# Expert tiles of a mixture-of-experts kernel: projections in native fp32 on two halves of the array, without splits

## What is computed

```python
D_MODEL, SEQ, N_EXPERTS, TOP_K_EXPERTS, EXPERT_FF = 1024, 256, 32, 2, 512
for e in range(N_EXPERTS):
    hid = jax.nn.silu(t @ w_gate[e]) * (t @ w_up[e])
    out = out + combine[:, e:e + 1] * (hid @ w_down[e]).astype(F32)
```

## Time and profile before

| | |
|---|---|
| median of three runs (least, most) | 2270.79 us (2269.74, 2271.43) |
| span of the profiled execution; its own time is not given apart | 2268.9 us |
| PE busy | 2194.2 us, 97% |
| DVE busy | 1573.7 us, 69% |
| ACT busy | 1168.7 us, 52% |
| POOL busy | 90.1 us, 4% |
| moved by DMA | 496.88 MB, mean 219 GB/s |

### The profile page before, as it was taken

The page is one execution under the profiler, slowest core; times in us unless marked ns, Lnnn a source line. Parts: engine busy times, 40 slices in busy tenths (PEclk is TensorE's granted clock), DMA queues, the critical chain, the costliest instruction groups (busy, mean ns, idle before and its releaser), DMA issues.

```text
span 2268.9 us, 26611 instructions
## 1 busy us (share of the span) xinstructions
PE 2194.2 (97%) x9804; PEld 1610.6 (71%) x9804; DVE 1573.7 (69%) x1576; ACT 1168.7 (52%) x1185; POOL 90.1 (4%) x79
## 2 busy tenths in 40 slices
PE   7989996999999999999999999999999999999999
PEld 5435765655665665565888887888888888878887
DVE  6989558888888878886555883855465558756554
ACT  4124524676666666665433585553354346665332
POOL 2750000000000000000000000000000000000000
PEclk9989997999999999999999999999999999999999
DMA  6224343999999999995555543555455544435653
GB/s 235 93 75 135 108 178 134 353 371 361 358 364 365 369 361 363 366 367 217 194 195 167 172 159 117 204 186 171 164 192 197 195 159 162 155 130 169 205 183 112
DMA packets 166451, 496.88 MB, mean 219 GB/s; under 512 B 10272, under 2 KB 21792, under 8 KB 136400
## 3 DMA queue, kind: packets, MB, share of 16 engines
q1 hardware_dynamic: 164528, 491.70, 60.8%
q10 hardware_dynamic: 1616, 3.24, 0.4%
q0 software_dynamic: 208, 0.59, 0.1%
HBM read 494.45 MB, written 1.05 MB: 218 GB/s over the span
## 4 chain that ended last, share of the span: by engine, by line
PE 82%; DVE 11%; issue 3%; ACT 3%; POOL 0%; DMA 0%; DVEq 0%; ACTq 0%; POOLq 0%
PE ps L1025 20%; PE ps L1035 15%; PE ps L1034 15%; PE ps L1511 9%; PE ps L1492 5%; PE ps L1496 5%; PE ps L1193 3%; PE ps L1480 2%; PE ps L1549 1%; DVE W_r L2859 1%; DVE xn L2582 1%; PE ps L1161 1%; PE ps L1162 1%; DVE W L2587 1%; ACT w_hi L2051 1%
## 5 line engine op out<-in xcount | busy, mean ns | idle before, releaser
L2398 DVE TENSOR_TENSOR w_lo<-raw,w_hi 128x2048 fp32r<-128x2048 f32 (+2 forms) x153 | 336.1, 2208 | 136.6 <-ACT w_hi L1830 129.4
L1830 ACT ACTIVATE w_hi<-raw 128x2048 fp32r<-128x2048 f32 (+2 forms) x153 | 281.6, 1849 | 227.3 <-PE ps L1025 194.1
L1035 PE MATMUL ps<-w_hi,a_lo 128*128 128x512 f32 (+1 forms) x984 | 371.6, 378 | 0.0
L1025 PE MATMUL ps<-w_hi,a_hi 128*128 128x512 f32 (+1 forms) x936 | 356.9, 381 | 0.2 <-DVEq L2438 0.2
L1034 PE MATMUL ps<-w_lo,a_hi 128*128 128x512 f32 (+1 forms) x928 | 349.5, 377 | 0.0
L1035 PEld LDWEIGHTS ps<-w_hi,a_lo 128*128 128x128 f32 x984 | 185.2, 188 | 34.6
L1025 PEld LDWEIGHTS ps<-w_hi,a_hi 128*128 128x128 f32 x936 | 176.2, 188 | 33.1 <-issue 2.1
L1034 PEld LDWEIGHTS ps<-w_lo,a_hi 128*128 128x128 f32 x928 | 174.8, 188 | 30.8
L1492 PE MATMUL ps<-w_hi,W_r 128*128 128x512 f32 x468 | 189.5, 405 | 4.3 <-DVE raw_r L2859 3.4
L2398 DVE TENSOR_TENSOR y_lo<-raw,y_hi 128x2048 fp32r<-128x2048 f32 x51 | 116.9, 2291 | 51.2 <-ACT y_hi L1830 48.6
L1830 ACT ACTIVATE y_hi<-raw 128x2048 fp32r<-128x2048 f32 x51 | 97.8, 1917 | 72.7 <-PE ps L1025 63.1
(11 more groups left out here) (468 smaller groups left out, 4325.5 us busy)
## 6 DMA issues: line engine op xcount, KB each, us to landing
raw<-in_w_in SPq DMA_DIRECT2D x56, 1024.0 KB, 5.1
raw<-in_ffn_w_gate SPq DMA_DIRECT2D x44, 1024.0 KB, 5.1
raw<-in_ffn_w_up SPq DMA_DIRECT2D x44, 1024.0 KB, 5.1
raw<-in_ffn_w_down SPq DMA_DIRECT2D x40, 1024.0 KB, 6.2
raw<-in_w_up SPq DMA_DIRECT2D x30, 1024.0 KB, 8.2
raw<-in_w_gate SPq DMA_DIRECT2D x30, 1024.0 KB, 7.2
lo_f<-in_w_up SPq DMA_DIRECT2D x30, 1024.0 KB, 8.1
lo_f<-in_w_down SPq DMA_DIRECT2D x29, 1024.0 KB, 7.9
```

Source lines behind the costliest of these rows:

```text
L1025: return released(pe.matmul(dst, a, b, skip_group_check=True, **kw))
L1035: return pe.matmul(dst, a_l, b_h, start=False, stop=final, skip_group_check=True)
L1830: act.activation(E.hi_view(name, ahead), E.raw_view(name, ahead), ACT.Copy).then_inc(hi_split, 1)
L2398: tt(E.lo_view(name, ahead), E.raw_view(name, ahead), E.hi_view(name, ahead).bitcast(F32), ALU.subtract)\
```

## The change

Gate and up are computed as down is: native fp32 products straight from the raw units. The 512 columns of a unit's block are cut in two halves of 256; the first goes to rows 0 to 63 of the bank and the second to rows 64 to 127, with the same 64 stationary columns at array position 0 and 64. Gate and up share one bank (columns 0 to 255 and 256 to 511). Down does the same with its two halves of 512 columns. All splits of expert weights go, and with them `lower_half` and `halves_added`. sil_e and hid_e become 128 rows of 256; two transposes turn them. A period gathers two blocks in one bank with one copy. `spread` and the output parts have two buffers, cleared once by POOL, and a tile is scattered two periods later (PE: `scatter_before`). Loads follow the order gate, up, down of one tile; the count of 8 buffers and of units stays.

```diff
-MOE_RAW, MOE_HI = 8, 4
+MOE_RAW = 8
...
+            def expert_gate_up(k, name, group, q):
+
+                dst = bank(name)
+                for i, kind in enumerate("gu"):
+                    for half in range(2):
+                        w = landed(((kind, k), half))
+                        for j in range(4):
+                            a = packed_rows[group][:, 4 * half + j, q, :]
+                            for side, rows in enumerate((lower_rows, upper_rows)):
+                                at = 512 * j + SEQ * side
+                                m = pe.matmul(dst[rows, SEQ * i:SEQ * i + SEQ], a, w[:, at:at + SEQ],
+                                              start=i == half == j == 0, stop=i == half == 1 and j == 3,
+                                              skip_group_check=True, tile_position=(0, SLOTS * side))
+                        if (kind, half) != ("u", 1):
+                            m.then_inc(expert_used, 1)
+                fill(m, name)
...
+                    w = landed((("d", k), half))
+                    for r in range(2):
+                        for c, rows in enumerate((lower_rows, upper_rows)):
+                            at = r * D + c * 512
+                            m = pe.matmul(dst[rows], hidT[:, r, half, :], w[:, at:at + 512], start=half == r == 0,
+                                          stop=half == r == 1, skip_group_check=True, tile_position=(0, SLOTS * c))
...
+            def scatter_before(k, acc):
+
+                scatter(marks["spread"].number(k, regs) - 1,
+                        lambda c: marks["out_split"].number((k, c), regs) - 3, acc, k[1] % 2).then_inc(done["scattered"], 1)
...
             def period(k, acc):
...
+                turn_expert(k)
+                if has_gather(k):
...
+                    gather(("G", k), i)
+                scatter_before(k, acc)
+                if has_next(k):
+                    if (q + 1) % GROUP_TILES == 0:
+                        pe.wait_ge(done["gathered_act"], nth("gathered_act", (which, q - 1)))
+                    expert_gate_up(k, ("gu", k), (q + 1) // GROUP_TILES % 2, (q + 1) % GROUP_TILES)
                 pe.wait_ge(done["expert_turned"], nth("expert_turned", k))
+                expert_down(k, releases=has_next(k))
...
-            expert_rounded(("g", "first"), 0)
             act.wait_ge(done["residual"], nth("residual", ("wo", 0, 1)))
...
-            expert_lower(("g", "first"), 0)
             gained_columns(0)
-            expert_lower(("g", "first"), 1)
             residual_part(1, 0)
...
+                if has_gather(k):
+                    gathered_copy(("G", k), k, (q + 1) % GROUP_TILES, ((q + 1) // GROUP_TILES + 1) % 2)
+                if has_next(k):
+                    gated(k, ("gu", k))
+                act.wait_ge(done["scattered"], nth("scattered", k))
+                act.wait_ge(bank_filled[bank_of[("y", k)]], fills(("y", k)))
                 output_rounded(k, 0)
                 output_rounded(k, 1)
...
+            pool.wait_ge(done["rows"], nth("rows", ("m", 1, 1)))
+            for q in range(2):
+                pool.memset(spread[q].bitcast(F32), 0.0).then_inc(zeroed, 1)
+                for c in range(2):
+                    pool.memset(out_parts[q][:, c, :].bitcast(F32), 0.0).then_inc(zeroed, 1)
             pool.wait_ge(done["residual"], nth("residual", ("wo", 1, 1)))
```

More of the change, by code:

```diff
@@ L121, in plan @@
 def plan():
[L123 removed]
+    units, shape, tiles = Order(), {}, Order()
     marks = {s: Order() for s in SIGNALS}
@@ L361, in plan @@
     fill("ranks", 6); fill("token_rows", 7); fill("slot_weights", 6)
[L362 to L374, removed]
+    for i in range(KB // 2):
+        fill(("G", "first", 0, i), i)
+        mark("gathered_act" if i % 2 else "gathered", ("first", 0, i))
+    expert_unit(("g", "first")); expert_unit(("u", "first"))
+    fill(("gu", "first"), 0)
+    fill(("G", "first", 1), 3)
+    mark("gathered_act", ("first", 1))
+    mark("gated", "first"); mark("expert_hidden", "first")
+    mark("spread", ("none", 0), ("none", 1))
+    mark("out_split", *(("none", q, c) for q in range(2) for c in range(2)))
     for c in range(2):
@@ L869, in bass_hybrid_moe_then_swa_gla, with has_next, has_gather @@
         stretch1 = straight(("u", 0), (("wo", 1), 1))
-        FIRST_TILES = [("g", "first"), ("u", "first"), ("g", "second")]
-        def period_units(k):
+        def has_next(k):
             which, q = k
-            up, gate = which == "loop" or q < EXTRA_TILES - 1, which == "loop" or q < EXTRA_TILES - 2
-            return [("u", k)] * up + [("d", k)] + [("g", k)] * gate
-        def next_units(k):
+            return which == "loop" or q < EXTRA_TILES - 1
+        def has_gather(k):
             which, q = k
[L879 to L889, removed]
+            return which == "loop" or q < GROUP_TILES - 1
         def periods(which):
@@ new lines, in scatter @@
+            def scatter(spread_value, split_value, acc, parity, columns=range(2)):
+                pe.wait_ge(done["spread"], spread_value)
+                for c in columns:
+                    pe.wait_ge(done["out_split"], split_value(c))
+                    for t in range(2):
+                        m = pe.matmul(acc[t][c], spread[parity][:, t * P:t * P + P], out_parts[parity][:, c, :], start=False,
+                                      stop=False, skip_group_check=True)
+                return m
@@ L3014, in pair_weights @@
                 dve.wait_ge(vector_step, step.next())
-                dve.memset(hid_e[SLOTS:P], 0.0).then_inc(vector_step, 1)
-                dve.wait_ge(vector_step, step.next())
             def places():
@@ L3162, in period @@
                     .then_inc(done["spread"], 1)
                 dve.wait_ge(done["spread"], nth("spread", k))
[L3164 to L3172 removed]
+                if which == "loop" and q % GROUP_TILES == 2:
+                    picked(k, column(regs["moe"] * 2 + (q // GROUP_TILES + 2)))
```

447 lines of the change are left out of this document (144 added, 303 removed).

## The result

The changed kernel takes 2175.14 us (median of 4 runs, 2172.4 to 2176.65) against 2270.26 (2268.06 to 2271.43) for the kernel before, run beside it: ratio 0.958, 95% interval 0.957 to 0.959, 95 us less. The forecast was 2190 with a range of 2160 to 2240. The profiled execution took 2175.44, with a span of 2173.5. Some steps of the sum came out otherwise, and TensorE stopped in two places that the forecast does not have.

The account below looks back on a forecast made before the run. PE bound the expert tiles (16.94 us), loads right behind; afterwards loads would, at 15.5 us. First feed-forward product at 982 plus 1206.3 untouched gives a 2188 us span, plus 2 to the median: 2190 us, range 2160 to 2240.

Parts of the forecast that it names:

- Pairs: Expert tiles on PE: two products on the array's halves cost one, so a tile needs 12.8 us instead of 16.94.
- not side by side: Third rival, expert tiles: a pair costs two products, 23.3 us a tile, time near 2498 us; chance 0.05.
- PE keeps the lead: Second rival, expert tiles: each pair takes 0.58 us in long streams, 15.6 to 17 us a tile; chance 0.09.
- The rate: Expert loads set the pace at 405 GB/s, 2.59 us a unit, 15.5 us a tile; bounds 380 and 420.
- The row of 10 us with 420: Old profile at 328 to 338 us, just after four units were issued: 420 GB/s, taken as the upper bound.
- The first rival: Expert loads go no faster, 361 to 380 GB/s, time 2229 to 2261 us; chance 0.14 for 361 to 390.
- The start: Start of the expert load stream: ninth unit issued at 376.9 us instead of 378.60, loop's first period at about 385.
- The end: End of expert stage: last unit at 964, late feed-forward units, their splits and lower part, first feed-forward product at 982 us.
- The clock kept at 1.0: PE's clock in the expert stage: waits near 1 us each, PE busy 8 of 10, so no slowdown was counted.
- Nothing for the splits and for the scatter: Expert tiles: removing weight splits, which PE hid, and scattering two tiles later were each worth nothing by themselves.

Follow-up runs that it names:

- half loads: The changed kernel with each expert unit loading 512 of its 1024 KB and PE reading the loaded half twice: 2114.69 us.
- the experiment on one half: The changed kernel with both 256-column halves of every gate and up product at array position 0, rows 0 to 63: 2384.95 us.

## Why the prediction was right, and where it was off

- **Pairs.** Right: 12.8 us a tile where the loads leave PE alone (12.81 with half loads; 12.76, from 382.43 to 395.19, for the changed kernel's first tile). Of the rivals, "not side by side" is refuted by the experiment on one half, which gave the loss that it foretold in kind (19.7 us a tile, as only gate and up were undone). "PE keeps the lead" is refuted by the step of 0.219 us in a stream of 32 passes. The rule of the Trainium skill (TensorE: Matmul & The Clock Gate, Packing small matmuls), by which a weight load overlaps only where the row group differs, does not agree with this trace: here all products share the rows, and 32 passes with their weight loads take 3.50 us.
- **The rate.** The mechanism was right, the size was not: 405 GB/s was taken between bounds of 380 and 420, and the stage ran at 419, 421 to 422 away from the stops. The row of 10 us with 420 was the answer, not the best case. From 374.17 to the landing of the last expert unit near 949.2 (2.5 before 951.7) it took 575 us, less 2, by 226: 2.54 us a unit instead of 2.59, stops included. That is 12 of the 17 us by which the first feed-forward product came sooner than forecast. (The landing at 949.2 is an estimate. The 2 us are the forecast's own; from its 5.1 less 2.5 it should have been 2.6, which changes the rate by less than 0.01 us a unit.) The first rival, the loads at 361 to 380, would have needed the dips to come from the transfers; they came from too few of them outstanding. The Trainium skill's 358 GB/s for HBM (DMA: Bandwidth & Descriptors, Where 436 GB/s comes from) disagrees with 419 over 550 us; its other figure, about 425 for a core that streams alone (HBM Reference, Specifications (TRN2)), agrees.
- **The start.** The ninth unit went out at 374.17, forecast 376.9: PE began on the first unit 4.3 us earlier (372.04 instead of 376.33), where 1.2 of the 4.6 us of splits was counted. The gather products ahead of it began 3.7 us earlier (365.81 instead of 369.51); the other 0.6 us was won in them, since fewer of them ran at the slower 0.63 us a pair. Using the unit took 2.1 us instead of 1.75. The loop began at 382.43, forecast 385.
- **The end.** The chain was named correctly, units landing, roundings, subtractions, lower part; the two units landed 2.5 us apart instead of 3, and from the second landing to the first feed-forward product it was 10.9 us instead of 11.8. 965.1 instead of 982: 2.7 from the start, 12 from the rate, 2 from here.
- **The clock kept at 1.0** was wrong in two places: after the stop (0.55 in 500 to 510 us) and after the 6 us of idle at the end, which gave back 2.1 us. The forecast had this idle time in its own sum and did not ask what it does to the clock.
- **Missed**: the stops at the loop's jumps, 3 to 6 us each. They and the better rate have opposite signs; without its stop the profiled run would have missed the forecast by some 18 to 21 us, so a few microseconds of its nearness are luck.
- **Nothing for the splits and for the scatter.** For the scatter right as the bound stands (2177.9 against 2176.64 us). That the splits alone were worth nothing before is read from PE's 4.8 us of waits in 400; no run took out them alone. Together with the products that replace theirs they become worth some 50 us once the down projection's pairs are in, and the scatter's delay 26 us once the loads no longer set the pace.

## What to carry to other kernels

Two native fp32 products of 64 columns of weights on the two halves cost one, also in long streams; that makes native fp32 from raw weights as cheap as split one-pass products (7.0 against 7.5 us a tile for gate and up, with 64 rows) and frees the engines that split. When a stage turns from compute to loads, its rate is not that of the old stage: take it from a stretch in which loads are queued, and count how many are outstanding before and after. Buffers past the number that fills the DMA engines most likely still pay, as the reserve that carries the stream over a stop.

## What had not been expected of the hardware

The load rate as a function of the 1-MB loads allowed on the way: three 329 GB/s, four 378, five 416, eight 419. And in the changed kernel PE stopped twice within 6 us, by 4 to 5 us each, at one of the jumps back of a loop of some 770 recorded passes (8 x 96), with the granted clock at 0.55 behind it and packets on the instruction queue only at the jumps that stop; loops of 512 to 520 passes had no such stop in the kernels profiled here.
